# A mixture-of-experts block: the order of the experts, four staging places for five, and a shorter activation

## What is computed

```
logits = h @ router_w + router_b                    # 1024 tokens, 32 experts
top_v, top_i = top_k(logits, 4);  gates = softmax(top_v)
# the 4096 assignments are sorted by expert into blocks of one expert each
gu   = xblk @ w_gu[e] + b_gu[e]                     # 1024 x 2048 weights, fp32
gate = minimum(gu[:, ::2], 7.0)
up   = clip(gu[:, 1::2], -7.0, 7.0)
act  = (up + 1.0) * gate * sigmoid(1.702 * gate)
y    = act @ w_down[e] + b_down[e]                  # 1024 x 1024 weights, fp32
out  = x + mod * rmsnorm(sum over the 4 experts of gate_value * y)
```

## Time and profile before

| | us |
|---|---|
| median of 3 runs | 2953.12 |
| lowest, highest | 2951.31, 2955.78 |
| profiled execution | 2952.93 |
| its span, first to last instruction | 2950.8 |

### The profile page before, as it was taken

The page is one execution under the profiler, slowest core; times in us unless marked ns, Lnnn a source line. Parts: engine busy times, 40 slices in busy tenths (PEclk is TensorE's granted clock), DMA queues, the critical chain, the costliest instruction groups (busy, mean ns, idle before and its releaser), DMA issues. The chain is left out here.

```text
span 2950.8 us, 133334 instructions
## 1 busy us (share of the span) xinstructions
PE 2602.3 (88%) x55873; PEld 2254.5 (76%) x55873; DVE 1820.0 (62%) x2096; ACT 1544.8 (52%) x1833; POOL 742.6 (25%) x586
## 2 busy tenths in 40 slices
PE   8999996998989896799999999999998899876662
PEld 2444556888878554799999999999998898876662
DVE  2344885445454487343525557766778888788995
ACT  3522543433433545243524556656667777777784
POOL 1211003535445012112222222222222323221121
PEclk9999998999999996899999999999999999998996
DMA  9400001000000325433525667776878989899997
GB/s 368 176 29 31 1 1 37 25 18 18 25 17 12 111 108 225 176 110 118 162 63 198 199 199 248 262 256 231 271 260 313 328 317 335 314 328 391 401 351 245
DMA packets 124475, 536.72 MB, mean 182 GB/s; under 512 B 12540, under 2 KB 13552, under 8 KB 91616
## 3 DMA queue, kind: packets, MB, share of 16 engines
q1 hardware_dynamic: 107120, 481.80, 44.2%
q0 software_dynamic: 14464, 47.79, 7.2%
q10 hardware_dynamic: 2832, 6.37, 0.6%
HBM read 496.99 MB, written 38.92 MB: 182 GB/s over the span
## 5 line engine op out<-in xcount | busy, mean ns | idle before, releaser
L2188 PE MATMUL ps<-qkv,weights 128*128 128x64 f16 x10496 | 958.6, 194 | 127.0 <-DVE weights L1679 57.6
L2188 PEld LDWEIGHTS ps<-qkv,weights 128*128 128x128 f16 x10496 | 931.8, 99 | 146.4 <-DVE weights L1679 68.1
L2189 PE MATMUL ps<-qkv,weights 128*128 128x64 f16 x10496 | 957.8, 194 | 1.8 <-issue 1.8
L2190 PE MATMUL ps<-qkv,weights 128*128 128x64 f16 x10496 | 957.8, 194 | 0.0
L2189 PEld LDWEIGHTS ps<-qkv,weights 128*128 128x128 f16 x10496 | 932.8, 99 | 1.9 <-issue 1.9
L2190 PEld LDWEIGHTS ps<-qkv,weights 128*128 128x128 f16 x10496 | 932.9, 99 | 0.0
L1679 DVE SCALAR_TENSOR_TENSOR weights<-hT,weights 128x2048 f16<-128x2048 f32 x256 | 591.3, 2365 | 148.8 <-ACT weights L1146 140.5
L1146 ACT ACTIVATE weights<-hT 128x2048 f16<-128x2048 f32 x256 | 521.7, 2093 | 86.9 <-DMA hT<-in_w_gu_dram 67.8
L2205 PE MATMUL ps<-qkv,weights 128*128 128x64 f16 x5248 | 472.0, 193 | 20.8 <-DVE weights L1684 19.7
L2205 PEld LDWEIGHTS ps<-qkv,weights 128*128 128x128 f16 x5248 | 461.5, 98 | 25.5 <-DVE weights L1684 24.3
L2206 PE MATMUL ps<-qkv,weights 128*128 128x64 f16 x5248 | 471.7, 193 | 0.0
(11 more groups left out here) (393 smaller groups left out, 4116.0 us busy)
## 6 DMA issues: line engine op xcount, KB each, us to landing
hT<-in_w_gu_dram SPq DMA_DIRECT2D x256, 1024.0 KB, 7.0
qkv<-in_w_down_dram SPq DMA_DIRECT2D x128, 1024.0 KB, 6.3
weights<-in_w_ada_dram SPq DMA_DIRECT2D x12, 2048.0 KB, 15.1
qkv<-in_w_in_dram SPq DMA_DIRECT2D x4, 2048.0 KB, 8.3
hT<-decay_rows SPq DMA_DIRECT2D x20, 256.0 KB, 3.5
hT<-beta_rows SPq DMA_DIRECT2D x20, 256.0 KB, 4.0
qkv<-in_x_dram ACTq DMA_DIRECT2D x8, 512.0 KB, 6.6
weights<-in_w_in_dram SPq DMA_DIRECT2D x2, 2048.0 KB, 14.0
```

Source lines behind the costliest of these rows:

```text
L2188: pe.matmul(dst, ghi[k][:, b, c], xT[:, 0, k, :], start=first, stop=False, skip_group_check=True)
L2189: pe.matmul(dst, ghi[k][:, b, c], xT[:, 1, k, :], start=False, stop=False, skip_group_check=True)
L2190: last = pe.matmul(dst, glo[k][:, b, c], xT[:, 0, k, :], start=False, stop=end, skip_group_check=True)
```

## The change

It has four parts.

- **Order of the experts.** An expert's place is no longer its rank but the lesser of 2·rank and 63 - 2·rank, worked out by four more small DVE instructions.
- **Staging.** `GS` is 4: chunk k of gate-and-up stands in place k mod 4, chunks 0 to 3 are loaded ahead, chunks 4 to 7 when low half 0, 1, 2, 3 is made; the loads ahead wait for low halves 4 to 7 and go to place 0, 1, 2, 3 for every expert.
- **One order of halves.** ACT makes high halves 0 to 4, copies x, makes half 5, does the activation, makes halves 6 and 7. DVE makes low halves 0 to 3, reads and activates, makes 4 to 7. `new0` is used no more. The waits that stand in for halves of an old expert are made in one step of eight.
- **Activation.** Gate and up are read in one DVE instruction of 128x1024. ACT does `Silu(ALPHA / WSCALE * gate)`, which has the gate's factor in it, so the product of up and gate (L1727) goes; the constants move to the scale of the result's copy.

```diff
-GS = 5
+GS = 4
...
-                    for k in AHEAD:
-                        sp.wait_ge(s_glo, t * GK + (k + GS + 1 if k + GS < GK else k + 1))
+                    for k in range(GS):
+                        sp.wait_ge(s_glo, t * GK + (GK - GS + k + 1))
                         sp.sem_inc(s_idle, 1)
                         gate_up_chunk(e, k)
...
-            AHEAD = (3, 4, 0, 1, 2)
...
             def sigmoid(t):
                 act.wait_ge(s_gc, t + 1)
-                act.activation(sig_n, gate_n, ACT.Sigmoid, scale=ALPHA / WSCALE).then_inc(s_sig, 1)
+                act.activation(sig_n, gate_n, ACT.Silu, scale=ALPHA / WSCALE).then_inc(s_sig, 1)
...
                     name_rows(t + 3)
-                    next_gate_up(t + 2, new2 > 0, r2, FIRST)
-                    next_gate_up(t + 2, new2 > new0, r2, PAIR)
+                    next_gate_up(t + 2, new2 > 0, r2, range(5))
                     copy_xT(t + 2)
-                    next_gate_up(t + 2, new2 + new0 > 1, r2, PAIR)
+                    next_gate_up(t + 2, new2 > 0, r2, range(5, 6))
                     sigmoid(t + 1)
-                    next_gate_up(t + 2, new2 > 0, r2, LAST)
+                    next_gate_up(t + 2, new2 > 0, r2, range(6, GK))
                     next_down(t + 1, new1 > new2, r1)
...
+            link(dve.tensor_scalar(mirror, rankcol, -2.0, float(2 * NE - 1), ALU.mult, ALU.add))
+            link(dve.scalar_tensor_tensor(placecol, rankcol, 2.0, mirror, ALU.mult, ALU.min))
             dve.wait_ge(s_ord, 2)
-            link(dve.tensor_scalar(before_of, ps[0:NE, 7, 0:NE], rankcol, None, ALU.is_gt))
+            link(dve.tensor_scalar(keys, ps[0:NE, 7, 0:NE], -2.0, float(2 * NE - 1), ALU.mult, ALU.add))
+            link(dve.scalar_tensor_tensor(places, ps[0:NE, 7, 0:NE], 2.0, keys, ALU.mult, ALU.min))
+            link(dve.tensor_scalar(before_of, places, placecol, None, ALU.is_gt))
...
-                dve.tensor_tensor(gate_n, gate, bias[:, bass.ds(e * 16, 8)].unsqueeze(2).to_broadcast([P, 8, B]), ALU.add)
-                dve.tensor_tensor(up_n, up, bias[:, bass.ds(e * 16 + 8, 8)].unsqueeze(2).to_broadcast([P, 8, B]),
+                dve.tensor_tensor(gate_up_n, both, bias[:, bass.ds(e * 16, 16)].unsqueeze(2).to_broadcast([P, 16, B]),
                                   ALU.add).then_inc(s_gr, 1)
...
                 chain(dve.tensor_scalar(up_n, up_n, LIMIT * WSCALE, -LIMIT * WSCALE, ALU.min, ALU.max))
-                dve.wait_ge(s_gc, t + 1)
-                chain(dve.scalar_tensor_tensor(up_n, up_n, WSCALE, gate_n, ALU.add, ALU.mult))
                 dve.wait_ge(s_sig, t + 1)
                 reached(dve, s_al, t, 1, 1)
-                chain(dve.scalar_tensor_tensor(act_n, up_n, 1.0 / (WSCALE * WSCALE), sig_n, ALU.mult, ALU.mult))
+                chain(dve.scalar_tensor_tensor(act_n, up_n, WSCALE, sig_n, ALU.add, ALU.mult))
...
-                    next_gate_up(t + 2, new2 > 0, r2, FIRST, 2)
-                    next_gate_up(t + 2, new2 > new0, r2, PAIR)
+                    next_gate_up(t + 2, new2 > 0, r2, range(4), GK)
                     read_gate_up(t + 1, e)
                     swiglu(t + 1)
-                    next_gate_up(t + 2, new2 + new0 > 1, r2, PAIR)
-                    next_gate_up(t + 2, new2 > 0, r2, LAST, 6)
+                    next_gate_up(t + 2, new2 > 0, r2, LAST)
                     next_down(t + 1, new1, r1)
```

More of the change, by code:

```diff
@@ L221, in hybrid_block @@
             QK[:], [D, 512, 512, 512, 512, 512, 512, 512, D])
+        gate_up_n = QK[:, D + 512:2 * D + 512].rearrange("p (c t) -> p c t", c=16)
         xg = xg.bitcast(F16)
@@ L269, in hybrid_block @@
         active = HT[0:NE, 1408:1408 + NB]
-        before_of, busier, keys = (HT[0:NE, 1536 + i * NE:1536 + (i + 1) * NE] for i in range(3))
-        keycol, rankcol = (HT[0:NE, 1664 + i:1665 + i] for i in range(2))
+        before_of, busier, keys, places = (HT[0:NE, 1536 + i * NE:1536 + (i + 1) * NE] for i in range(4))
+        keycol, rankcol, mirror, placecol = (HT[0:NE, 1664 + i:1665 + i] for i in range(4))
         startf, usedf, lessf = HT[0:NE, 1280:1281], HT[0:NE, 1281:1282], HT[0:NE, 1282:1283]
@@ L417, in hybrid_block @@
         s_gc = sem("gate_clamped")
-        s_sig = sem("gate_sigmoid_ready")
+        s_sig = sem("gate_silu_ready")
         s_a = sem("activation_ready")
@@ L518, in hybrid_block @@
         MINB = SEQ * TOPK // B
-        FIRST, PAIR, LAST = range(2), range(2, 4), range(4, GK)
+        LAST = range(4, GK)
         @block.sync
@@ L655, in _ @@
             for i in range(GS):
-                sp.wait_ge(s_gst[i], last * 32 + 32 if i + GS < GK else last * 16 + 16)
-                if i < DK:
-                    sp.wait_ge(s_dst[i], last * 16 + 16)
+                sp.wait_ge(s_gst[i], last * 32 + 32)
+                sp.wait_ge(s_dst[i], last * 16 + 16)
                 sp.sem_inc(s_idle, 1)
@@ L1139, in flags_and_ranks @@
                 code = act.value_load(code_of[0:1, bass.ds(t, 1)], min_val=0, max_val=256 * NE - 1)
-                new0, new1, new2, r1 = code & 1, (code >> 1) & 1, (code >> 2) & 1, ((code >> 3) & (NE - 1)) + 1
-                return new0, new1, new2, r1, r1 + new1
+                new1, new2, r1 = (code >> 1) & 1, (code >> 2) & 1, ((code >> 3) & (NE - 1)) + 1
+                return new1, new2, r1, r1 + new1
             def high_gate_up(t, r, k):
-                act.wait_ge(s_gst[k % GS], (r * 2 + (k // GS)) * 16 + 16 if k % GS + GS < GK else r * 16 + 16)
+                act.wait_ge(s_gst[k % GS], (r * 2 + k // GS) * 16 + 16)
                 reached(act, s_gu, t, GK, k + 1 - GK)
@@ L1188, in copy_yT @@
                 act.activation(yT, ps[:, BT, :].rearrange("p (c t) -> p c t", c=8), ACT.Copy,
-                               scale=1.0 / WSCALE).then_inc(s_yT, 1)
+                               scale=1.0 / (ALPHA * WSCALE * WSCALE)).then_inc(s_yT, 1)
             def scale_y(t):
@@ L1260, in _ @@
                 with act.If(t <= nprev):
-                    new0, new1, new2, r1, r2 = flags_and_ranks(t)
+                    new1, new2, r1, r2 = flags_and_ranks(t)
                     act.wait_ge(s_xg, t * 16 + 48)
@@ L1695, in next_gate_up @@
                     with dve.Else():
-                        dve.wait_ge(s_glo, t * GK + part[-1] + 1 - old)
+                        dve.wait_ge(s_glo, t * GK + part[0])
                         dve.sem_inc(s_glo, old)
@@ L1705, in next_down @@
                     dve.sem_inc(s_dlo, DK)
-            chain = Chain(dve, s_chain, 3)
+            chain = Chain(dve, s_chain, 2)
             def expert(t):
@@ L1712, in read_gate_up @@
             def read_gate_up(t, e):
-                gate, up = (ps[:, b, :].rearrange("p (c t) -> p c t", c=8) for b in (BG, BU))
+                both = ps[:, BG:BG + 2, :].rearrange("p b (c t) -> p (b c) t", c=8)
                 bias = btab.rearrange("p e j -> p (e j)")
```

## The result

| | before | after |
|---|---|---|
| median, us | 2953.22 | 2991.7 |
| lowest, highest | 2951.31, 2955.78 | 2990.54, 2994.03 |
| span of the profiled execution | 2950.8 | 2992.3 |
| clock over the span | 0.959 | 0.951 |
| DVE busy | 1820.0 | 1763.4 |

The change makes the kernel 1.3% slower: ratio 1.0131, 95% interval 1.0113 to 1.0148, four runs of each. The forecast was 2965, slower by 12 us; it is slower by 38.5.

What follows compares the result with a forecast made beforehand. PE sets the pace for the first two thirds, then is short of weights. From a span of 2950.8, +36.3 for switches, -25.0 end and +0.8 start give 2962.9, with 2.1 around it 2965 us; own range 2943 to 2985.

Steps and rivals of the forecast that it cites:

- 13 quiet exits: Switches leaving an expert of three or more blocks: the load lands almost in time, 0.3 us lost each.
- 9 pairs: Switches leaving a two-block expert: x and activation wait for half 4's late load, 9.1 us lost each.
- 9 singles: Switches leaving a one-block expert: x and activation wait for load 4, 11.25 us lost each.
- over the pitch, against 150.75: Expert loop's time beyond 18.75 us a block: 187.1 us over all switches, where the old kernel had 150.75, so +36.3.
- end: After block 81 starts: its weights are there, so the first last scatter leaves 20.9 us earlier, the next 4.1 more: -25.0.
- start: Routing before the loop: four more small DVE instructions, +0.8 us.
- a sign against it: In the expert loop: the forecast is wrong if PE waits at quiet switches; no size given.
- the walk: Step-by-step timing of a switch from the old expert's last block; the quiet one ends at 29.9, where the pitch wants 29.95.
- Activation and Silu: Each block's activation: some 0.8 us less DVE work, hidden or swallowed by waits; Silu costs nothing, no table load.
- The clock: PE's slower clock after waiting for x at exits: taken as 0, at most 2.2 us an exit.
- Single exits keep their old price: Rival, leaving one-block experts: 14.4 us each because DMA is the bound, 28 more, 2993 us in all; chance 0.12.
- the wider one: Whole kernel's time: the forecast's range stretched towards the first and second rival, 2925 to 2994 us.

Runs made afterwards that it cites:

- e2: The changed kernel with the experts in the old order of rank: 3027.36 us, ratio 1.0245 to the kernel before.
- e12: The changed kernel with the down weights' high halves behind the rounded activation where block t is a new expert too: 2983.44 us, ratio 1.0106.
- e6: The kernel before with the shorter activation alone (one merged read, Silu, one product less): 2965.4 us, ratio 0.9997.
- e9: The changed kernel, four places, with x and activation behind high half 3 and down high halves behind the rounded activation at exits: 2902.21 us, ratio 0.9833.
- e11: The changed kernel with down high halves behind the rounded activation at exits, x and activation behind half 2, DVE likewise: 2907.29 us, ratio 0.9836.
- e3: The changed kernel, four places kept, with ACT copying x and doing the activation behind high half 3: 2920.1 us, ratio 0.9892.
- e4: The changed kernel with five staging places, its new order of halves kept: 2927.84 us, ratio 0.9920.
- e5: The changed kernel with five places and x and activation behind high half 3: 2948.94 us, ratio 0.9936.
- e7: The changed kernel with five places, x and activation behind high half 3, down high halves behind the rounded activation at exits: 2924.73 us, ratio 0.9855.
- e8: The changed kernel with only half of each gate-and-up chunk loaded after the first expert's: 2943.65 us, ratio 0.9931.

## Why the forecast was right in sign and short in size

By its own steps, in us of the profiled span:

| term | forecast | measured |
|---|---|---|
| 13 quiet exits | 3.9 | 3.2, for the four into a pair |
| 9 pairs | 9 x 9.1 = 81.9 | 64.2 = 9 x 7.1 |
| 9 singles | 9 x 11.25 = 101.3 | 144.1 = 9 x 16.0, with the nine quiet exits into them |
| over the pitch, against 150.75 | +36.3 | +60.8 |
| end | -25.0 | -20.8 |
| start | +0.8 | +1.5 |
| sum | +12.1 | +41.5 |

**Quiet exits.** The load came as worked out: in all 13 it is 4.9 to 5.1 us from SP's issue to ACT's half 4 (2041.67 and 2046.60 at the switch into the single above, 12.2 after the block's start). By the 6.15 us for 1 MB of the Trainium skill (DMA: Bandwidth & Descriptors, "Measured (HBM→SBUF, 128 partitions, SWDGE, issued from GpSimd)") they would have lost, by the forecast's estimate, 15.6 in all; the trace disagrees with it here too. But the loss isn't 0.3. The four exits into a pair lose 0.6 to 1.1 each, and in e2, where all 13 can be told apart, it is 10.0 in all. PE does wait at quiet switches, which the forecast had named as a sign against it. What the walk left out is a gap of 0.7 us between DVE's last step of the activation and its next low half: it is in the earlier trace rows, where 2431.34 stands 0.75 behind the end of the step, and in no walk. At the quiet exit from 2612.7 on:

```profile
2630.47 0.69 DVE L1729 SCALAR_TENSOR_TENSOR qkv<-qkv 128x512 f32<-128x512 f32 x1 [2.25 <-ACT qkv L1177]
2631.85 9.86 DVE L1681 SCALAR_TENSOR_TENSOR weights<-hT,weights 128x2048 f16<-128x2048 f32 x4 [0.68 <-DVE qkv L1729]
```

DVE's step ends 18.5 after the block's start, for 18.6 in the walk, but the halves end at 29.1 for 28.5, and the exit loses 0.6.

**Pairs.** The mechanism held: x and the activation behind half 4, the load 10.6 us after its issue (11.1 in the working). That exit lost 8.8, of 9.1 forecast. The mean is 7.1 (5.4 to 8.8), because the load is not always that late: from issue to copy it takes 6.7 to 10.6, 8.2 in the mean, and at 2464.55 ACT waited only 4.28 for it. One exit of the kernel before was taken for nine, and its 11.1 is later than any of them.

**Singles: the step that failed** is the last of that walk: "66.0, and PE's last down chunk 1.5: 67.5, against 3·18.75 = 56.25. Loss 11.25." Up to there it was nearly sound: load 4 came at 41.7 for 41.0, the activation's end at 47.1 for 46.7. Two things are wrong with the rest. First, the walk is 1.6 short at its own end: DVE's last step ends 47.9 for 47.4, then comes the gap of 0.68 that was left out, so the eight halves end at 67.2 for 66.0, and the block after starts 1.9 behind them and not 1.5, at 69.1. In the mean of the nine (67.3 us lost in the singles' own blocks, 51.7 in the ones behind) 119.0/9 = 13.2 is lost by then, for 11.25: 17.8 us. Second, and larger, the walk stops there. It takes the exit to be over after the single's down products and does not ask what is late next: the next expert's down chunks. Their loads can be issued only when the single's down halves are made, and ACT takes them ahead of the rounded activation. Each of the nine exits loses 1.3 to 4.3 in one more block for this, 25.1 in all, and e12 takes it to 0. Together these are the 42.9 that were short. The earlier trace rows could not show the place, since before all singles came last, one behind another.

**End.** The first of the last scatters goes 21.7 after block 81 starts, where 21.3 was worked out; 42.2 before. That gave 20.5 of 20.9. Of the other 4.1 next to nothing came. They supposed that the next scatter waits for the first (8.73 before). The first is quick now, 4.4, as supposed, but the next is issued 10.45 us behind it and was 10.97 before, because now it waits for PE, which stands at 7.12 us of "issue" where its loop ends.

**Activation and Silu** held: hidden (e6), no table load in the loop.

**The clock.** I took 0 for it. The granted clock is 0.96, 0.91 and 0.93 in the three blocks of the exit above, and 0.80 from 1328 to 1353, after PE had waited for x; in the next expert's first block PE is busy 21.26 us, and 18.52 in block 81. No run separates its cost from the waits that hide it: in e9 PE is busy 21.36 at clock 0.90 and in e11 20.08 at 1.00 for the same block, and both end at the same time.

**The rivals.** "Single exits keep their old price", 2993, was nearest in time (2991.7): a single cost 14.4 before and costs 16.0 now. But its reason, DMA as the bound, is not what the runs show: with all bytes unchanged, e3 brings singles from 144.1 to 100.3. The forecast's own range ended at 2985; 2991.7 is inside the wider one, by 2 us, only because that was stretched for this rival. That is luck, and so is a second thing: the pairs came 17.7 cheaper than forecast and so hid part of what the singles were short.

The sizes of the four parts, then: the order alone 1.0019; with it the new order of halves and the activation, on five places, 0.9920; the fifth place taken away, 1.0131. The step from the second to the third, 62 us, is the change's whole loss.

## What to carry to other kernels

Where a buffer's place is reused within one round, look at what else stands behind the instruction that needs the second use, on its engine's queue. Here the copy of x and the activation, 1.6 us of work that needs no weights, behind one late copy made a loss of 1.3% of what is a gain of 1.1% when they stand ahead of it. Follow an exit until every stream of loads has caught up, not until the first engine is free: the down chunks were the next thing late. And give a remedy its price together with the others: the fifth place was worth 62 us behind the bad order (changed kernel, e4) and by the ratios nothing behind the good one (e3 and e5, e9 and e7). And put the small gaps between two dependent instructions into a walk: here 0.7 us was left out at every exit.

## What the runs showed of the hardware

Half the bytes didn't halve a load's time: from issue to ACT's copy at a quiet exit 1 MB took 4.9 to 5.1 us in the changed kernel and 512 KB 3.6 to 3.9 in e8; at a pair's exit, behind the down loads, 8.2 and 7.1 in the mean of nine. Four 1 MB loads in a row reach ACT 2.5 to 2.6 us apart here (2106.50, 2109.04, 2111.59, 2114.10). The second chip ran a quiet block 0.1 to 0.3 us slower than the others (read in e6; on the other two a quiet block takes 18.75), with the same granted clock of 0.96 over the span: 2966.68 for 2953.41 in the kernel before, 0.45%.
